# Score blocks within 32 tokens as 32x32 tiles in four column groups

## The reference, cut to what matters

```
S_t = diag(f_t) S_{t-1} + k_t v_t^T ,   o_t = S_t^T q_t
scores[t, s] = sum over d of q[t,d] * exp(b[t,d] - b[s,d]) * k[s,d]   for s <= t     (b = cumsum of log f)
o[t] = sum over s of scores[t, s] * v[s]   (+ the part of the state)
```

## Time and profile before

| what | value |
|---|---|
| time, median of 3 runs (lowest to highest) | 851.43 us (851.15 to 852.05) |
| time of the profiled execution | 850.92 us |
| its span, first to last instruction | 849.0 us |
| busy share of the span: PE, DVE, ACT, POOL | 98%, 80%, 68%, 20% |
| chain that ended last, by engine | PE 93%, DVE 3%, ACT 2% |
| share of the score line L1523 in that chain | 2% |
| mean transfer rate over the span | 262 GB/s |

### The profile page before, as it was taken

One profiled execution on the slowest core, in us unless ns is written; L12 is line 12 of the kernel. 1 busy time (PEld: TensorE's weight loads), 2 busy tenths in 40 slices (PEclk: granted clock), 3 DMA queues, 4 the chain that ended last, 5 costly groups with the idle time before them and its releaser, 6 DMA issues.

```text
span 849.0 us, 14351 instructions
## 1 busy us (share of the span) xinstructions
PE 832.6 (98%) x5471; PEld 726.6 (86%) x5471; DVE 681.3 (80%) x837; ACT 574.1 (68%) x715; POOL 169.5 (20%) x147
## 2 busy tenths in 40 slices
PE   6999999999999999999999999999999999999996
PEld 6999999999999999999988777777777777777776
DVE  5899678777665547996888889898998989898964
ACT  6857765544544348577966878787878787787842
POOL 4430276555411132303800000000000000000001
PEclk9999999999999999999999999999999999999998
DMA  8843267555678526424495999999999999899911
GB/s 301 313 159 108 78 236 253 186 185 173 245 276 274 194 100 209 139 100 176 161 310 177 384 381 421 322 408 338 395 376 355 391 344 414 320 422 323 395 66 52
DMA packets 52404, 222.01 MB, mean 262 GB/s; under 512 B 6208, under 2 KB 6336, under 8 KB 51694
## 3 DMA queue, kind: packets, MB, share of 16 engines
q1 hardware_dynamic: 50670, 209.61, 67.4%
q0 software_dynamic: 960, 9.50, 3.0%
q10 hardware_dynamic: 720, 2.18, 0.6%
HBM read 214.25 MB, written 7.47 MB: 261 GB/s over the span
## 4 chain that ended last, share of the span: by engine, by line
PE 93%; DVE 3%; ACT 2%; issue 1%; DMA 1%; DVEq 0%; ACTq 0%
PE bank L1812 43%; PE bank L1498 12%; PE bank L1499 12%; PE bank L1500 12%; PE bank L1656 2%; PE bank L1523 2%; PE bank L1868 2%; PE bank L1784 1%; PE bank L1821 1%; DVE sb_w_lo L997 1%; ACT sb_w_hi L570 1%; DMA sb_raw<-in_in_units_dram 1%; PE bank L1581 0%; PE bank L1749 0%; PE bank L1648 0%
## 5 line engine op out<-in xcount | busy, mean ns | idle before, releaser
L997 DVE TENSOR_TENSOR sb_w_lo<-sb_raw,sb_w_hi 128x1024 fp32r<-128x1024 f32 (+1 forms) x116 | 173.6, 1497 | 61.7 <-ACT sb_w_hi L570 60.5
L1498 PE MATMUL bank<-at_act_hi,sb_w_hi 128*128 128x264 f32 x672 | 194.1, 289 | 8.1 <-DVE sb_w_lo L997 8.1
L570 ACT ACTIVATE sb_w_hi<-sb_raw 128x1024 fp32r<-128x1024 f32 (+1 forms) x116 | 127.1, 1101 | 96.0 <-PE bank L1500 94.0
L1499 PE MATMUL bank<-at_act_lo,sb_w_hi 128*128 128x264 f32 x672 | 191.5, 285 | 0.0
L1500 PE MATMUL bank<-at_act_hi,sb_w_lo 128*128 128x264 f32 x672 | 191.3, 285 | 0.0
L1812 PE MATMUL bank<-sb_w_hi,at_packed 128*96 128x512 f32 (+1 forms) x768 | 189.7, 375 | 0.2 <-DVE at_packed L1264 0.2
L1044 DVE TENSOR_TENSOR sb_w_lo<-at_raw_e,sb_w_hi 128x1408 fp32r<-128x1408 f32 (+1 forms) x112 | 159.7, 1447 | 27.0 <-ACT sb_w_hi L638 26.4
L638 ACT ACTIVATE sb_w_hi<-at_raw_e 128x1408 fp32r<-128x1408 f32 (+1 forms) x112 | 139.0, 1242 | 38.2 <-PE bank L1812 38.2
L1044 DVE TENSOR_TENSOR sb_w_lo<-sb_raw,sb_w_hi 128x1408 fp32r<-128x1408 f32 (+1 forms) x104 | 149.8, 1479 | 14.3 <-ACT sb_w_hi L638 14.3
L1812 PEld LDWEIGHTS bank<-sb_w_hi,at_packed 128*96 128x96 f32 x768 | 122.4, 161 | 38.1 <-DVE at_packed L1264 0.6
L638 ACT ACTIVATE sb_w_hi<-sb_raw 128x1408 fp32r<-128x1408 f32 (+1 forms) x104 | 130.3, 1259 | 32.7 <-PE bank L1812 32.5
(11 more groups left out here) (275 smaller groups left out, 1255.7 us busy)
## 6 DMA issues: line engine op xcount, KB each, us to landing
sb_raw<-in_moe_w_up_dram SPq DMA_DIRECT2D x36, 704.0 KB, 7.2
at_raw_e<-in_moe_w_down_dram SPq DMA_DIRECT2D x49, 512.0 KB, 7.0
at_raw_e<-in_moe_w_gate_dram SPq DMA_DIRECT2D x35, 704.0 KB, 9.2
sb_raw<-in_up_units_dram SPq DMA_DIRECT2D x44, 512.0 KB, 3.3
sb_raw<-in_moe_w_gate_dram SPq DMA_DIRECT2D x29, 704.0 KB, 9.2
sb_raw<-in_in_units_dram SPq DMA_DIRECT2D x39, 512.0 KB, 3.8
sb_raw<-in_moe_w_down_dram SPq DMA_DIRECT2D x39, 512.0 KB, 5.2
at_raw_e<-in_moe_w_up_dram SPq DMA_DIRECT2D x28, 704.0 KB, 6.2
```

Of the source, the lines that this page charges most:

```text
L570: act.activation(w_hi[s][:, 0:kts, :], raw[s][:, 0:kts, :], ACT.Copy).then_inc(hi_done, 1)
L997: dve.tensor_tensor(w_lo[s][:, 0:kts, :], raw[s][:, 0:kts, :], w_hi[s][:, 0:kts, :].bitcast(f32), ALU.subtract).then_inc(lo_done, 1)
L1498: pe.matmul(out[:, 0:T], w_hi[s][:, k, :], hi[:, c, :], start=(c == 0), stop=False)
L1499: pe.matmul(out[:, 0:T], w_hi[s][:, k, :], lo[:, c, :], start=False, stop=False)
```

## The change

Products 0 to 6 pair tokens that lie within the same 32. So they are computed as the four diagonal 32 x 32 blocks alone: for each head and block one matmul with a stationary of 32 columns and 32 moving columns, whose result goes to the 32 partitions of that block (`tile_position`, one of four column groups). A product is then 16 matmuls instead of four, and its result 128 partitions x (4 heads x 32). The takes copy this compact form under masks of 32 columns into a new tile `near` (three parts: the two diagonals, and `both`), and `part_scores` stays within `near`. The two segments' compact blocks are put in place in `scores` by ACT: four copies of 32 x 128 for each segment, written behind put(5) and put(6) (`put_near`). PE waits for five puts instead of three. The masks in the constants shrink from 8 x 128 columns to 8 x 32. Products 7 to 9 stay as they were.

```diff
@@ POOL
-                gp.memset(both[:, :, :], 0.0).then_inc(scores_zeroed, 1)
+                gp.memset(near[:, :, :, :], 0.0).then_inc(scores_zeroed, 1)
@@ ACT
                     if (it, s) in PUTS:
                         put(PUTS[(it, s)])
+                        if PUTS[(it, s)] < len(LEVELS):
+                            put_near(PUTS[(it, s)] - MARKED)
...
+                def put_near(seg):
+
+                    act.wait_ge(scores_zeroed, 2 * (L + 1))
+                    for b in range(SEG // NEAR):
+                        block = slice(NEAR * b, NEAR * (b + 1))
+                        done = act.activation(scores[block, seg, :, block], near[block, seg, :, :], ACT.Copy)
+                    done.then_inc(scores_put, 1)
@@ DVE
                 def mask(n):
-                    return consts[:, C_MASK + 128 * n:C_MASK + 128 * (n + 1)].bitcast(i32).unsqueeze(1).broadcast_to([128, HEADS, SEG])
+                    return consts[:, C_MASK + NEAR * n:C_MASK + NEAR * (n + 1)].bitcast(i32).unsqueeze(1).broadcast_to([128, HEADS, NEAR])
...
-                    src = bank[score_bank(i)][:, :].rearrange("p (h t) -> p h t", h=HEADS)
+                    src = bank[score_bank(i)][:, 0:HEADS * NEAR].rearrange("p (h t) -> p h t", h=HEADS)
...
-                    dst = scores[:, i, :, :] if i < 2 else both[:, :, :]
-                    dve.copy_predicated(dst, mask(max(i - 1, 0)), src).then_inc(scores_taken, 1)
+                    dve.copy_predicated(near[:, min(i, 2), :, :], mask(max(i - 1, 0)), src).then_inc(scores_taken, 1)
...
-                        dve.copy_predicated(scores[:, seg, :, :], mask(1 + MARKED + seg), both[:, :, :]).then_inc(scores_taken, 1)
+                        dve.copy_predicated(near[:, seg, :, :], mask(1 + MARKED + seg), both).then_inc(scores_taken, 1)
@@ PE
                     for h in range(HEADS):
-                        mm = pe.matmul(bank[score_bank(i)][:, 128 * h:128 * (h + 1)], left(h), right(h), start=True, stop=True)
+                        if i >= MARKED + 2:
+                            mm = pe.matmul(bank[score_bank(i)][:, 128 * h:128 * (h + 1)], left(h, slice(0, SEG)), right(h, slice(0, SEG)), start=True, stop=True)
+                            continue
+                        for b in range(SEG // NEAR):
+                            block = slice(NEAR * b, NEAR * (b + 1))
+                            mm = pe.matmul(bank[score_bank(i)][block, NEAR * h:NEAR * (h + 1)], left(h, block), right(h, block), start=True, stop=True,
+                                           tile_position=(0, block.start))
                     mm.then_inc(scored, 1)
...
-                pe.wait_ge(scores_put, 3 * (L + 1))
+                pe.wait_ge(scores_put, 5 * (L + 1))
```

More of the change, by code:

```diff
@@ L30 @@
 MARKED = 5
+NEAR = 32
 LATE = 1
@@ L39 @@
 C_MASK = 512
-C_CORR = C_MASK + 128 * (1 + len(LEVELS))
+C_CORR = C_MASK + NEAR * (MARKED + 3)
 C_PICK = C_CORR + 4 * PAD
@@ L174, in build_program @@
         hg_tmp = at("hg_tmp", [128, HEADS, T], 80512)
-        both = at("both", [128, HEADS, SEG], 81024)
+        near = at("near", [128, 3, HEADS, NEAR], 81024)
+        both = near[:, 2, :, :]
         sample_kq = at("sample_kq", [128, HEADS, DEC], 80512)
@@ L1530, in score_level @@
                         pe.wait_ge(keys_done, 2 * L + 1)
-                        score(0, lambda h: k[:, h, 0:SEG], lambda h: q[:, h, 0:SEG])
+                        score(0, lambda h, t: k[:, h, t], lambda h, t: q[:, h, t])
                         pe.wait_ge(keys_done, 2 * (L + 1))
-                        score(1, lambda h: mirrored_keys[:, h, :], lambda h: q[:, h, SEQ - 1:SEG - 1:-1])
+                        score(1, lambda h, t: mirrored_keys[:, h, t], lambda h, t: q[:, h, SEQ - 1 - t.start:SEQ - 1 - t.stop:-1])
                         return
@@ L1538, in score_level @@
                     z = sided[j % 2]
-                    score(j + 2, lambda h: z[:, 0, h, :], lambda h: z[:, 1, h, :])
+                    score(j + 2, lambda h, t: z[:, 0, h, t], lambda h, t: z[:, 1, h, t])
                 PE_LEVELS = {(2, 1): -1} | {divmod(10 + LATE * (1 - L) + j, 4): j for j in range(len(LEVELS) + 1)}
@@ L1939, in constants @@
     c[:, C_IOTA:C_IOTA + 128] = i[None, :] + 1
[L1940 to L1946, removed]
+    s, t = i[:, None] % NEAR, np.arange(NEAR)[None, :]
+    masks = [s == t] + [(s // (2 * half) == t // (2 * half)) & (s // half != t // half) for half in LEVELS[:MARKED]] + [s < t, s > t]
+    for n, m in enumerate(masks):
+        c[:, C_MASK + NEAR * n:C_MASK + NEAR * (n + 1)] = m
     for g, w in enumerate(WINDOWS):
```

## The result

The changed kernel took 852.92 us (median of 12 runs, 851.52 to 853.45) where the kernel before took 851.36 (median of 12): a ratio of 1.0017, with the interval 1.0010 to 1.0024, or 1.5 us slower. The profiled execution took 853.29 us with a span of 851.2. The forecast was 851.4, no change. All medians here are of fast runs alone, which leaves out one run of 2899.81 us of a later kernel.

What follows compares the result with a forecast made beforehand. PE carried 93% of the chain of waits; layer 0's +0.28 and layer 1's -0.33 summed to -0.05 us, giving 850.9 for the profiled execution and a forecast median of 851.4. The range was 848.6 to 855.0.

Steps and rivals of the forecast that it cites:

- PE's passes: Mixer scores on PE: 32 passes, four column groups side by side, 0.58 us instead of 0.89; PE gains 3.2 a layer.
- The third rival: Score tiles on PE don't run side by side: sum +6.9, 858.3 us, or near 880; chance 0.11.
- DVE's copies: Nine masked copies a layer on DVE, each 0.22 us instead of about 0.63, a gain of 0.40 each.
- the five takes: Layer 0's takes where GpSimd's diff subtraction runs: shorter takes only let DVE's split stand longer, so they gain nothing.
- the first rival: DVE's gain counts in full, layer 0 -1.7 and layer 1 -1.34: sum -3.0, 848.4 us; chance 0.21.
- ACT's copies: Eight near copies a layer behind put(5) and put(6) on ACT, 0.29 us each, 2.34 a layer; bounds 0.20 and 0.32.
- layer 0's end: Layer 0's last w_hi copy, DVE's drain and PE's transposes: -2.06 + 2.34 = +0.28 us.
- Layer 1: Layer 1's last w_hi copy and pool_lo: -0.96 - 1.71 + 2.34 = -0.33 us.
- PE's gain is spent in that wait: Layer 0, before the transposes: PE's gain of 3.2 us goes into waiting for DVE's drain, with no further cost counted.
- the second rival: The clock falls when PE stands still some 3.5 us before layer 0's transposes: 2.4 us lost, 853.8; chance 0.14.
- The prediction's own sign of being wrong: Granted clock below 1 near 85 us, or layer 0's transposes starting before 84.0 or after 87.
- the same sum: Both layers' mixer ends added, other edits at nothing: +0.28 - 0.33 = -0.05 us.

Runs made afterwards that it cites:

- the filler: Changed kernel plus eight fp32 matmuls of 264 columns on PE behind layer 0's third pool matmul, result unread: 851.64 us, ratio to before 1.0004.
- blocks by DVE: Changed kernel without ACT's near copies; DVE's masked copies write the 32x32 blocks straight into place, put(5) and put(6) don't wait for the takes: 852.27 us.
- changed, later levels: Changed kernel with layer 1's levels one step later on DVE, ACT and PE, as in layer 0: 854.44 us, ratio 1.0039.
- before with copies: Kernel before plus eight 32x128 copies on ACT in layer 0, into a spare tile nobody reads, no tiles: 855.34 us, ratio 1.0050.
- wait moved: Changed kernel, copies still on ACT, but only the near copies wait for the takes, not put(5) and put(6): 851.27 us, ratio 0.9997.
- no near copies: Changed kernel with ACT's eight near copies a layer left out, so scores are incomplete: 847.86 us, ratio 0.9958.
- GpSimd with the wait: Changed kernel with the near copies on GpSimd; put(5) and put(6) still wait for the takes: 846.88 us, ratio 0.9947.
- GpSimd, 0: Layer 0 of the changed kernel with near copies on GpSimd; put(5) and put(6) don't wait for the takes: 847.08 us, ratio 0.9951.

## Why the prediction was wrong

Its mechanisms on PE, DVE and ACT were right; the price of the stop that they make, which it had in a rival, was left out of its sum. The time, 852.92, lies inside its range, but it forecast no change (-0.05 us) where the kernel lost 1.5.

- *PE's passes:* right. A lone score went from 0.89 to 0.59 (forecast 0.58): from the last matmul of the unit before it, at 47.61, to the second behind it, at 48.44, are 0.83, less the 0.24 that two steps of 0.12 take with no score between. Its 32 passes start within 0.26 us (forecast 0.24). The level behind read_states went from 2.09 to 1.49, a gain of 0.60 (forecast 0.65). The third rival is out. The Trainium skill's rule against the change (TensorEngine Tiling (Array Packing), "Instruction Overhead": some 60 cycles a matmul) would have given 1.14 a score, by the prediction's estimate; the measured 0.59 decides, and the rule did not hold for these passes, which go to four column groups in turn.
- *DVE's copies:* right. Two takes in 0.49, part_scores 0.50; the split beside GpSimd's subtraction took 2.52 instead of 1.67 and ended 1.07 us behind that subtraction, as before (1.08). Subtraction and split both came 0.32 earlier than before, and no more than that later in the layer, so the five takes gained nothing and the first rival is out.
- *ACT's copies:* 0.32 each instead of 0.29, the upper bound; 2.58 a layer instead of 2.34 (eight of 0.29 are 2.32, a slip that changes nothing). Counted from the later start, put(5) came 2.2 earlier (forecast 2.06), so layer 0's end was +0.36 (forecast +0.28).
- *Layer 1:* +0.14 instead of -0.33: the copies' 0.24, and ACT's wait of 0.32 for PE's small sum, which had been early enough before. A mis-sized term of half a microsecond.
- *"PE's gain is spent in that wait":* this is the step that failed. The sum put the stop at nothing, and left its price to the second rival, with a chance of 0.14. In its place the trace shows a stop of 3.83 us in which the granted clock fell to 0.50, and 2.1 us lost behind it. The rival had sized both: a stop of some 3.5 us and 2.4 us lost. Against it the prediction set only that the stretch before the fall in the earlier trace rows "held other small work". But the trace of the kernel before has no stop among dense matmuls of more than 0.8 us, so no row showed that the clock would hold through one of 3.5. The prediction's own sign of being wrong, a granted clock below 1 near 85 us, came true. With the fall in place the same sum gives +0.36 + 2.1 + 0.14, and with the 0.2 of a later start and the 0.5 won later the +2.3 of the trace.

That the rival's 2.4 came so near is in part luck. It took 5.2 us at half clock from the kernel's start; here 5.2 us of matmuls ran at half clock, but behind four of the other stops it was 3.4 at most, and the loss 0.6 to 1.5.

The runs differ with the clock: the mean granted clock of the changed kernel's twelve runs goes from 0.995 in the fastest (851.52) to 0.992 in the profiled one (853.29); with the filler it is 0.995 to 0.997, as in the kernel before. So the median's loss is 1.5 and the trace's 2.3. How long the clock was low in the runs without a trace is not shown.

## What to carry to other kernels

Work taken off the bounding engine ahead of a wait that it can't move is not free time: here 3 us less matmul work in front of a fixed wait cost 1 to 2 us behind it, because in the stop TensorE's clock came down. Before such a cut, follow the wait's releaser to the engine that sets it, and move work off that engine first: the same eight copies a layer cost 6 us more on ACT than on idle GpSimd (852.92 against 846.88), of which the clock's part is about 1.1. Where the stop can't be closed, filler matmuls can hold the clock; here eight of them, 3.72 us in a stop of 3.83, did.

## What the runs showed of the hardware that was not expected

The stops and what the clock did, each from one profiled execution (blocks by DVE: before the first and the third pool matmul and before the transposes, with the fall ahead of the last):

| kernel, layer | PE's stop at the end of the mixer, us | half clock, us | lost behind it, us |
|---|---|---|---|
| changed, 0 | 3.83 | 84.05 to 90.88 | 2.1 |
| changed, later levels, 0 | 3.87 | 84.66 to 91.49 | 2.4 |
| changed, later levels, 1 | 3.42 | 388.45 to 391.86 | 1.5 |
| before with copies, 0 | 2.99 | 88.35 to 91.76 | 1.3 |
| wait moved, 0 | 2.76 | 85.42 to 88.83 | 1.3 |
| blocks by DVE, 0 | 0.48, 1.55, 0.48 | 84.12 to 87.53 | 0.6 |
| no near copies, 0 | 1.38 | none | 0 |
| GpSimd with the wait, 0 | 1.08 | none | 0 |
| GpSimd, 0 | 0.83 | none | 0 |

- The mean granted clock of the runs counted here agrees with the traces: it is 0.995 to 0.997 in the kernels whose trace has no fall (the one with the filler among them), and 0.990 to 0.995 in the others, but for three runs of "wait moved" with 0.996.
- The clock often fell late: behind the stops of 3.42, 2.99, 2.76 and 1.55 us it fell 0.2 to 0.9 us after PE had started again.
- What decides between the 1.38 us that left the clock at 1.00 and the 1.55 with a shorter stop ahead of it is not shown.
- A masked copy of 32 partitions x 128 took 0.31 us on DVE, one of 128 x 128 some 0.20 (the next instruction starts 0.40 behind the first of two).
- The Trainium skill (GPSIMD Engine Reference, "Key points") says that GpSimd shares its SBUF interfaces with VectorE and contends with instructions of two SBUF inputs. Beside GpSimd's subtraction the split does stretch, from 1.22 to 2.52; beside its 32-partition copies DVE's windows, which have two inputs as well, kept their 0.98, 0.71 and 0.43, and three shorter instructions behind them took 0.1 longer.
